# Weight splits put off, a mask load cut in two, and an input scale taken from weighted sums of squares, in a two-block transformer kernel on one Trainium2 core

## What is computed

```
# block 1
h = rms_norm(x, mix_norm_g); proj = h @ w_in      # 14 column groups, 4 attention kinds + gates
x = x + sum(sigmoid(gates) * (branches @ w_branch)) @ w_out
h = rms_norm(x, mlp_norm_g); x = x + relu(h @ w_up)**2 @ w_down
x = rms_norm(x, final_norm_g)                     # "final norm" of block 1, weight gF
# block 2
h = rms_norm(x, norm1_g_2); proj = h @ w_in_2     # q, k, v and a gated convolution branch
x = x + concat(attention, layer_norm(conv)) @ w_out_2
h = rms_norm(x, norm2_g_2); x = x + (silu(h @ w_gate_2) * (h @ w_up_2)) @ w_down_2
```

## Time and profile before

| what | value |
|---|---|
| median of 3 runs | 773.2 us (773.14 to 773.86) |
| profiled execution | 773.35 us, its span 771.5 us |
| PE busy | 760.8 us, 99% of the span |
| DVE busy | 582.8 us, 76% |
| ACT busy | 408.6 us, 53% |
| POOL busy | 49.3 us, 6% |
| granted TensorE clock | 1.00 over the span |

### The profile page before, as it was taken

The page is one execution under the profiler, slowest core; times in us unless marked ns, Lnnn a source line. Parts: engine busy times, 40 slices in busy tenths (PEclk is TensorE's granted clock), DMA queues, the critical chain, the costliest instruction groups (busy, mean ns, idle before and its releaser), DMA issues.

```text
span 771.5 us, 9633 instructions
## 1 busy us (share of the span) xinstructions
PE 760.8 (99%) x3712; PEld 636.2 (82%) x3712; DVE 582.8 (76%) x945; ACT 408.6 (53%) x555; POOL 49.3 (6%) x42
## 2 busy tenths in 40 slices
PE   8989999999999999999999999999999999999998
PEld 6878899888888888888888887888988888888886
DVE  5698688697757878687778838699857777768584
ACT  7666255456657546545454546764665344353430
POOL 0200000000001500000000005041000000000000
PEclk9999999999999999999999999999999999999999
DMA  9953434454544467665665567655133665655601
GB/s 334 391 175 110 136 110 142 159 168 161 163 164 164 159 204 249 192 216 175 208 205 179 173 207 273 218 172 164 56 110 109 222 215 181 200 184 199 206 13 54
DMA packets 68508, 137.28 MB, mean 178 GB/s; under 512 B 2544, under 2 KB 6256, under 8 KB 67824
## 3 DMA queue, kind: packets, MB, share of 16 engines
q1 hardware_dynamic: 68032, 135.30, 52.6%
q10 hardware_dynamic: 432, 1.38, 0.5%
HBM read 135.48 MB, written 1.05 MB: 177 GB/s over the span
## 4 chain that ended last, share of the span: by engine, by line
PE 85%; DVE 8%; DMA 3%; ACT 2%; SPq 1%; issue 1%; ACTq 0%
PE b L652 19%; PE b L654 18%; PE b L653 18%; PE SS L652 4%; PE SS L654 4%; PE SS L653 4%; DVE wlo L1605 2%; PE TT L621 2%; PE OO L652 2%; PE OO L654 2%; PE OO L653 2%; DMA cs<-in_cst 2%; DVE ca L2128 2%; DMA xr<-in_x 1%; PE b L814 1%; PE SS L761 1%
## 5 line engine op out<-in xcount | busy, mean ns | idle before, releaser
L1605 DVE TENSOR_TENSOR wlo<-raw,whi 128x2048 fp32r<-128x2048 f32 (+2 forms) x119 | 269.9, 2270 | 80.3 <-ACT whi L1144 79.5
L1144 ACT CAST whi<-raw 128x2048 fp32r<-128x2048 f32 (+2 forms) x119 | 222.9, 1878 | 124.4 <-PE b L654 81.9
L652 PE MATMUL b<-whi,Ahi 128*128 128x512 f32 (+2 forms) x520 | 206.7, 398 | 2.9 <-ACT gates L1217 2.4
L654 PE MATMUL b<-whi,Alo 128*128 128x512 f32 (+2 forms) x520 | 199.8, 384 | 0.0
L653 PE MATMUL b<-wlo,Ahi 128*128 128x512 f32 (+2 forms) x520 | 199.1, 383 | 0.0
L652 PEld LDWEIGHTS b<-whi,Ahi 128*128 128x128 f32 x520 | 97.8, 188 | 21.1 <-ACT gates L1217 2.9
L654 PEld LDWEIGHTS b<-whi,Alo 128*128 128x128 f32 x520 | 97.6, 188 | 19.9
L653 PEld LDWEIGHTS b<-wlo,Ahi 128*128 128x128 f32 x520 | 97.9, 188 | 17.8
L1993 DVE STREAM_TRANSPOSE hT<-ust 32x256 f32<-32x256 f32 (+1 forms) x192 | 81.5, 425 | 2.8
L652 PE MATMUL b<-whi,Bhi 128*128 128x512 f32 x154 | 60.5, 393 | 0.1
L654 PE MATMUL b<-whi,Blo 128*128 128x512 f32 x154 | 60.0, 390 | 0.0
(11 more groups left out here) (295 smaller groups left out, 1095.1 us busy)
## 6 DMA issues: line engine op xcount, KB each, us to landing
raw<-in_w_in SPq DMA_DIRECT2D x38, 1024.0 KB, 5.1
raw<-in_w_up SPq DMA_DIRECT2D x16, 1024.0 KB, 5.4
raw<-in_w_dn SPq DMA_DIRECT2D x16, 1024.0 KB, 5.1
raw<-in_w_d SPq DMA_DIRECT2D x11, 1024.0 KB, 5.0
raw<-in_w_g SPq DMA_DIRECT2D x10, 1024.0 KB, 5.0
raw<-in_w_u SPq DMA_DIRECT2D x10, 1024.0 KB, 5.1
raw<-in_w_out SPq DMA_DIRECT2D x8, 1024.0 KB, 5.1
raw<-in_w_br SPq DMA_DIRECT2D x4, 1024.0 KB, 5.0
```

The costliest lines, as they stand in the source:

```text
L652: e.matmul(dst, xh, H[:, kc, c0:ce], start=first and kc == krs[0], stop=False)
L654: ins = e.matmul(dst, xl, H[:, kc, c0:ce], start=False, stop=last and kc == krs[-1])
L1144: e.copy(whi[:, s, 0:m], raw[:, r, 0:m]).then_inc(s_hi, 1)
L1605: e.tensor_tensor(wlo[:, s, 0:m], raw[:, r, 0:m], whi[:, s, 0:m].bitcast(F32), ALU.subtract).then_inc(s_lo, 1)
```

## The change

It does five things.

1. The load of the tables MB, UO and LG is taken out of the large load, gets its own semaphore (d_cs0) and is issued one weight unit earlier. The second and fourth heads of the stick-breaking attention start one slot later (10 and 16 for 9 and 15).
2. `split_after` is put off for the units from the last of p2 on: from the first unit of wo2 up to the middle of the first g and u groups the split comes 2 to 5 groups ahead of first use instead of 6.
3. POOL's four multiplies by gF come after both roots and after all N2 squares and transposes. The scale r4 is no longer taken from a second round of four squares by ACT but by DVE: it multiplies the squares that are already in ys by gF^2 with a running sum (`square_sum`, four times 128x512). gF^2 is made once by ACT in the third up stage.
4. The multiply of xr by r3 goes away; the residual of wo2 does it in the same instruction.
5. Eight convolution taps move from the attention loop into p2: 2 more at each of slots 12, 14, 16 and 18.

```
-    for h, a in enumerate((8, 9, 14, 15)):
+    for h, a in enumerate((8, 10, 14, 16)):
...
-    for s, n in ((10, 8), (12, 2), (14, 4), (16, 3), (18, 3)):
+    for s, n in ((10, 8), (12, 4), (14, 6), (16, 5), (18, 5)):
...
             g = free_at[i - NSPL]
+        first = min(groups[t] for t in unit_of if unit_of[t] == i)
+        if i >= unit_of["p2", 4, 1, 0]:
+            g = max(g, first - {unit_of["p2", 4, 1, 0]: 6, unit_of["wo2", 0, 0, 0]: 5}.get(i, 2))
+            if i > unit_of["wo2", 1, 1, 0]:
+                g = max(free_at[i - NSPL], first - 3 - max(0, i - unit_of["u", 0, 0, 0]) // 2)
         g = max([g] + [h + 1 for h in split_after])
+        assert g <= first - 2, (i, g, first)
...
+            if i == NRAW + 3:
+                o = CST["MB"][0]
+                e.dma_start(cs1[:, o:N1], cst_d[:, N0 + o:N0 + N1]).then_inc(d_cs0, 16)
             if i == NRAW + 4:
                 e.dma_start(cst[:, 136:N0], cst_d[:, 136:N0]).then_inc(d_cs1, 16)
-                e.dma_start(cs1[:], cst_d[:, N0:N0 + N1]).then_inc(d_cs1, 16)
+                e.dma_start(cs1[:, 0:CST["MB"][0]], cst_d[:, N0:N0 + CST["MB"][0]]).then_inc(d_cs1, 16)
...
         def sc(h, s):
-            w.wait_ge(d_cs1, 32)
+            w.wait_ge(d_cs0, 16)
...
+                if j == 3 and q == 0:
+                    w.wait_ge(d_par2, 16)
+                    e.activation(g2row, par2[:, 0:1024], ACT.Square).then_inc(s_g2, 1)
...
-                    for t_, n_ in ORD:
-                        fin_square(t_, n_)
...
         def residual(base, t, n):
+            if base == 8:
+                e.scalar_tensor_tensor(out=xs, in0=xs, scalar=r3_[:, t:t + 1], in1=bank[W_ACC[t, n]], op0=ALU.mult,
+                                       op1=ALU.add).then_inc(s_res, 1)
+                return
...
+        def square_sum(t, n):
+            sq = ys[:, t, 512 * n:512 * n + 512]
+            w.wait_ge(s_g2, 1)
+            w.wait_ge(s_sq, SQ["N2", t, n] + 1)
+            return own(e.tensor_tensor_reduce(sq, sq, g2row[:, 512 * n:512 * n + 512], 1.0, 0.0, ALU.mult, ALU.add,
+                                              o4[:, 2 * t + n:2 * t + n + 1]))
 
         def stats2():
             stats("r3", o3, SQ["N2", 1, 1] + 1)
-            before("p2", 0, 0, 1)
+            square_sum(0, 1)
+            k = square_sum(1, 1)
...
             variance("r4", v, sm_, D)
-            for t in range(2):
-                ins = e.tensor_scalar(xr[:, t, :], xr[:, t, :], r3_[:, t:t + 1], None, ALU.mult)
-            k_x = own(ins)
+            before("p2", 0, 0, 1)
...
                     before("p2", 0, ui, t)
+                    square_sum(0, 0)
+                    square_sum(1, 0)
                     turn2(1, 1)
...
-            conv(6 if k < 4 else 4 if k < 8 else 1)
+            conv(4 if k < 8 else 1)
...
         w.wait_ge(d_par2, 16)
+        root("r3", r3_, smx["r3"][1], 2)
+        root("r4", smx["r4"][2], smx["r4"][1], 2)
+        w.wait_ge(s_sq, SQ["N2", 1, 1] + 1)
+        w.wait_ge(s_xt, XT["N2", 1, 1] + 1)
         for t, n in ORD:
             xs = xr[:, t, 512 * n:512 * n + 512]
-            w.wait_ge(s_sq, SQ["N2", t, n] + 1)
-            w.wait_ge(s_xt, XT["N2", t, n] + 1)
             e.tensor_tensor(xs, xs, par2[:, 512 * n:512 * n + 512], ALU.mult).then_inc(s_pg, 1)
-        root("r3", r3_, smx["r3"][1], 2)
-        root("r4", smx["r4"][2], smx["r4"][1], 2)
```

More of the change, by code:

```diff
@@ L253, in build @@
     d_xt = [sem(f"d_xt{i}") for i in range(5)]
+    d_cs0 = sem("d_cs0")
     d_x0, d_x1, d_par, d_cst, d_cs1, d_par2, d_tw, d_tw3, d_hp, d_out = [
@@ L286, in build @@
     s_pool = sem("s_pool_step")
+    s_g2 = sem("s_gfin_squared")
     s_warm = sem("s_warm")
@@ L422, in build @@
                                          + [("N2", t, n) for t, n in ORD]
-                                         + [("F", t, n) for t, n in ORD]
                                          + [("N3", t, n) for t, n in ORD])}
@@ L445, in build @@
     RT, RT2 = rope[:, 0, :], rope[:, 1, :]
+    g2row = PT2[:].rearrange("p a b -> p (a b)")
     NT, NSH = 4, 16
@@ L1405, in _ @@
                 relu2(j, 1)
-        def fin_square(t, n):
-            w.wait_ge(s_pg, ORD.index((t, n)) + 1)
-            square("F", t, n, xr[:, t, 512 * n:512 * n + 512], o4)
         def turn2(t, n):
@@ L2034, in _ @@
                 before("dn", 7, n, t)
+        def square_sum(t, n):
[4 more added lines that the diff above has]
+                                              o4[:, 2 * t + n:2 * t + n + 1]))
         def stats2():
             stats("r3", o3, SQ["N2", 1, 1] + 1)
-            before("p2", 0, 0, 1)
+            square_sum(0, 1)
+            k = square_sum(1, 1)
             sm_, v, r = smx["r4"]
             o4v = o4.rearrange("p (t n) -> p t n", n=2)
-            w.wait_ge(s_sq, SQ["F", 1, 1] + 1)
+            w.wait_ge(s_dve, k)
             w.wait_ge(s_rs, RS["r3"] + 1)
@@ L2049, in stats2 @@
             variance("r4", v, sm_, D)
-            for t in range(2):
-                ins = e.tensor_scalar(xr[:, t, :], xr[:, t, :], r3_[:, t:t + 1], None, ALU.mult)
-            k_x = own(ins)
+            before("p2", 0, 0, 1)
             w.wait_ge(s_rs, RS["r4"] + 1)
             e.tensor_tensor(r4_, r3_, r, ALU.mult).then_inc(s_rv, 1)
-            return k_x
         def r0(i):
@@ L2166, in _ @@
                     before("p2", 0, ui, t)
+                    square_sum(0, 0)
+                    square_sum(1, 0)
                     turn2(1, 1)
-                    k_x = stats2()
+                    stats2()
                 before("p2", i, ui, t)
@@ L2198, in ln @@
                                 ALU.mult).then_inc(s_lv, 1)
-        w.wait_ge(s_dve, k_x)
+        w.wait_ge(s_pg, 4)
         out_proj("wo2", "N3", 8, "g_n2")
```

## The result

The changed kernel takes 780.4 us in the median of 4 runs (778.08 to 780.76), against 773.4 for the kernel before: ratio 1.0083, 95% interval 1.0063 to 1.0103. It is slower, as forecast, but by 7.0 us and not by 2.6, and 2.4 us beyond the upper end of my range. In the profiled execution (780.34 us, span 778.2 against 771.5) the mean granted clock is 0.996, where the kernel before had 1.00.

The account below looks back on a forecast made before the run. PE, busy 99% of the span, was taken to bound the kernel. From 773.35, -2.6 - 0.6 + 2.4 - 0.9 + 4.5 gave 776.15, so 776.0 us for the median, range 774.0 to 778.0.

Parts of the forecast that it names:

- Key scaling: In p2, six more taps ahead of DVE's key scaling make PE wait 3.6 instead of 1.2 us: +2.4 us.
- Third group of wo2: Second half of wo2: unit 89's late subtraction stands behind the second residual, so PE waits: +3.4 of +4.5 us.
- the next two: Second half of wo2, after the third group: late splits of units 90 and 91 make PE wait, +0.3 and +0.7 us.
- Attention loop: With two subtractions and eight taps gone from DVE's work, gaps in the loop close: -0.9 us.
- End of block 1: PE's wait for an Alo at 476 us goes, as POOL's multiplies no longer run beside it: -0.6 us.
- The weighted sums: End of block 1: four added DVE sums of 128x512 take 0.75 us each, bounds 0.6 and 1.5.
- the first term: First projection: PE's wait at 41 to 43 us goes, as ACT's copy precedes the second head's functions: -2.6 us.
- Rival (a): wo2: late splits hide, unit 89's subtraction running before the second group ends; 771.5 us, chance 4%.
- Rival (b): p2: added taps cost nothing, the wait at 526 being ACT's or the root's; 772.8 to 773.6 us, chance 10%.
- Rival (c): After wo2's waits: queued casts of units 91 to 95 and late loads, or doubled weighted sums; +2.1, 778.1 us, 13%.

Follow-up runs that it names:

- x2: The changed kernel with 14 filler matmuls into an unused bank ahead of the third group of wo2's second half: 778.9 us.
- x3: The changed kernel with the old tap table (8, 2, 4, 3, 3 taps in the second projection, 6 per head for four heads, then 4): 780.2 us.
- x4: The kernel before with the masks' load in two and heads at slots 8, 10, 14, 16: 772.6 us; two runs 770.70 and 770.88, nine 772.11 to 773.26.
- x14: x4 with 8 instead of 6 warm-up matmuls: six runs at 770.33 to 771.07 us, six at 772.56 to 773.15.
- x1: The changed kernel with the splits of units 88 and 89 (second half of w_out2) put back earlier: 775.4 us.
- x15: The changed kernel with 8 warm-up matmuls and filler matmuls in both long waits, at the key scaling and in wo2: 776.6 us.
- x5: The kernel before with the rule for the late splits alone (from unit 85 on): 780.1 us.
- x10: The kernel before with the changed tap table alone (8, 4, 6, 5, 5 taps in the second projection, 4 per head in the loop): 776.2 us.
- x12: The changed kernel with 8 instead of 6 warm-up matmuls: 780.4 us.

## Why the prediction was wrong

**The direction and five mechanisms were right.** Key scaling: forecast 3.6 us of gap, measured 3.6 (net +2.4 both). Third group of wo2: forecast 3.4, measured 3.45 (3.80 us from the transposes to the group, 0.35 before); the next two forecast 0.3 and 0.7, measured 0.2 (0.3 in x2 and x3) and 0.6. Attention loop: forecast -0.9, measured -1.1. End of block 1: forecast -0.6, measured -1.0, since besides the gap of the earlier trace rows a smaller one of 0.2 us at 469 went. The weighted sums took 0.69 us, forecast 0.75. With POOL's multiplications moved, the subtraction that stood beside them takes 0.69 us and not 1.78. The rule of the Trainium skill, "SBUF — State Buffer", on the shared port pair, which the prediction weighed, agrees with that.

**What failed is the first term and a term that isn't there.**

- "I count the whole 2.6 us" for the first projection: I took the length of a wait in one execution for what its removal gives back. That execution had a quick start. The wait's end is set by a load and by ACT, so it swallows a slow start; without it most runs keep that loss. The runs of part one gave 0.7 instead of 2.6 (x4), and about the full amount (2.2 to 3.0 us) only in the eight runs of the lower groups of x4 and x14. In the changed kernel's profile the wait's removal gave 2.8 us and the slow start took 2.0: 0.8 in place of 2.6.
- The sum prices a wait at its own length. Behind the 3.4 us in wo2 the clock fell and cost 2.7 us more. The sentence "the granted clock is 1.00 throughout" was true of the kernel before and was no ground for one with longer waits (x1, x2).

The sum closes with these two: 776.15 + 2.0 (start) + 2.7 (clock) + 0.3 (outside the span), less the 0.8 us that the first projection, the end of block 1 and the attention loop gave beyond their forecasts (0.2, 0.4 and 0.2), is 780.35, and the profiled execution took 780.34. That x15 lies within half a microsecond of the forecast's sum is in part luck, since these small misses cancel.

**Right in size, incomplete in cause:** for the key scaling I wrote that the split put off by a slot changes nothing, since it stays ahead of the scaling on DVE. On DVE it does. On ACT its cast went in front of the square that DVE's sum needs, and this alone gives 2.66 us (x5). The number came out right because the taps fill that idle time (x10).

Rival (a) fell: the split waits behind the residual. Rival (b) fell for the kernel as changed, though its thought that ACT could be what holds the scaling came true in x3 and x5. Rival (c), casts and loads later on, fell: from 601 us to the last matmul the distance between the two traces grows by less than 0.1 us.

**Open:** why a run starts at full or at half rate, with the same kernel, and why the same wait is followed by half clock in one kernel and not in another. The Trainium skill, "TensorE: Matmul & The Clock Gate", says in "HAM oscillation — how this bites in real kernels" that idle gaps between matmuls let the clock fall back, and in "Part 1: The HAM clock gate" that the number of slow matmuls at a kernel's start varies from run to run. Nine of eleven waits and the two groups of x4 and x14 agree; I had not held the first of these rules against the wait that I forecast.

## What to carry to other kernels

Before counting a wait as gain, look at what sets its end: where that is a load or another engine, the wait also absorbs whatever varies ahead of it, and its removal pays only the part that is there in every run. And a wait that a change adds on a saturated TensorE costs more than its length once TensorE is idle as long as here: check the granted clock behind it, fill it if it can't be avoided, and first try to move one weight subtraction past the instruction that is waited for.

## What the runs showed of the hardware

- After waits of 2.65 to 3.46 us TensorE ran at half clock in nine cases of eleven; the granted clock read 0.50 for 3.4 to 6.8 us, at a cost of 1.4 to 2.7 us. The exceptions are the changed kernel's wait at 524 us (3.44) and x5's at 584 us (3.14). Behind waits up to 2.4 us (the kernel before) the clock stayed at 1.00. The length of the wait alone doesn't decide. The fall can also come late: in x3 the matmuls behind the wait start at 525.81, lie 0.23 us apart until 527.23 and 0.40 to 0.43 from there.
- Matmuls on dummy operands in the wait kept the clock up and delayed nothing (x2, x15).
- What is won early can be lost again to the clock: x12 came to the key scaling 1.8 us earlier than the changed kernel (525.70 against 527.45) and ended at the same time.
- The granted clock of the windows reads 1.00 up to 10 us in every trace, also where matmuls lie 0.43 us apart; at the start the spacing is to be read, not the clock.
